# Key search: operands of VectorE's long products in a PSUM bank, unit tiles over two banks instead of four

## Chip, cores and metric

The kernel runs on one core of a Trainium2 chip. The metric is the device time of one execution in microseconds (us), from three runs. A core has five engines here: PE (matmuls), ACT (ScalarE), DVE (VectorE), POOL (GpSimd), and SP, which only issues transfers. SBUF is the large on-chip memory. PSUM holds eight banks of 128 x 512 float32 values, into which PE writes.

## What is computed

The reference is a transformer-like block (attention, a state space branch, cross attention, a product-key expert layer, and a second block after it). The change lies in the expert layer:

```python
def peer_ffn(a, w_q, sub_keys, u_tab, v_tab):      # 256 tokens, d = 1024
    qry = (af @ w_q).reshape(n, PEER_HEADS, 2, PEER_KEY_DIM)              # 8 heads, 2 halves
    s = jnp.einsum('nhpd,hpkd->nhpk', qry, sub_keys)                     # 128 keys a half
    s_top, i_top = lax.top_k(s, PEER_TOPK)                               # best 16 of 128
    cand = (s_top[:, :, 0, :, None] + s_top[:, :, 1, None, :]).reshape(n, PEER_HEADS, 256)
    sc, ci = lax.top_k(cand, PEER_TOPK)                                  # best 16 of 256 pairs
    e_a = jnp.take_along_axis(i_top[:, :, 0], ci // PEER_TOPK, axis=-1)
    e_b = jnp.take_along_axis(i_top[:, :, 1], ci % PEER_TOPK, axis=-1)
    experts = e_a * PEER_N_KEYS + e_b
    gw = jax.nn.softmax(sc, axis=-1)
    ...  # act = gelu(u_tab[experts] . x);  out = sum (gw * act) * v_tab[experts]
```

The kernel doesn't gather experts. It computes the activation of all 16384 experts for all tokens, multiplies by a dense matrix of gates, and sums with all rows of v_tab.

## The kernel before

**Unit tiles.** The 16384 experts are 128 tiles of u_tab, 128 experts each. A tile is a weight of 128 x 1024 float32. It arrives in a ring of four slots (SP's transfers). To keep float32 precision it is split in two: ACT copies it to a rounded `w_hi` (`split_high`), and another engine forms the rest `w_lo` = tile - `w_hi` (`split_rest`). `w_hi` and `w_lo` have two buffers each. PE then does 24 matmuls for the tile (`split_channels`): 16 with `w_hi` ("high"), and 8 with `w_lo` ("rest"), before which it waits for the rest. ACT takes the result out of the PSUM bank with a Gelu (`unit_out`), and SP stores it to HBM.

**Three loops.** The unit tiles run as loop `u1` (52 tiles, `U_EARLY`), loop `u2` (64 tiles, between which PE also builds the gate matrix, job `w`), and loop `u3` (12 tiles). In `u1` the rests are made by POOL (line 834 of the profile), so that DVE is free for the key search. In `u2` and `u3` DVE makes them (line 2170). `plan_banks` fixes the bank of every PSUM job in advance, and the counts of fills and releases on which PE, ACT and DVE wait. In `u1` the tiles rotate over banks 4, 5, 6, 7, in `u2` over 4, 5. Before `u1`, the jobs `sk` (key scores) and `ce` use banks 4 to 7. After `u1` come `eTr` (the turned expert numbers and gates, banks 6 and 7) and `cH` (banks 4 and 5).

**Order on ACT in u1.** For each tile `unit_out` of tile j comes first and `split_high` of tile j + 2 next. After 48 tiles (`U_EXP`) ACT does two small exponentials for the gates (`gate_exp`), with a change of its function table on either side.

**The key search on DVE.** For each half t of the tokens: `best_keys(t)` finds the best 16 of 128 for 16 groups, `best_pairs(t)` adds them to 256 pairs a head (`CAND`), finds the best 16 of those, and turns their places into expert numbers by one-hot products of 2048 values a partition; `gate_scores(t)` subtracts the best score. Between `best_keys(0)` and `best_pairs(0)` DVE does one product for another branch (line 2625: `CKK` by `CEX`, 2048 values). `gates(t)` waits for ACT's exponentials. `step(...)` makes DVE wait for its own last instruction. All these operands stand in `arena`, which is SBUF; PSUM shows as `banks` in the profile. Line 2580 is the sum for `CAND`, line 2594 the comparison, line 2595 the product with the numbers, line 2596 the sum over the one-hot axis, line 2600 the subtraction in `gate_scores`.

Of the kernel before, what the change touches and what calls it, by code (L numbers as in the profile page):

```python
# [21 lines left out]
P = 128  # L22
# [18 lines left out]
PH, PK, PTOP = 8, 128, 16  # L41
# [10 lines left out]
ALU = mybir.AluOpType  # L52
# [82 lines left out]
U_EARLY, U_EXP, U_GATED = 52, 48, 64  # L135
# [65 lines left out]
def plan_banks():  # L201
    B = Banks()
# [52 lines left out]
    for k in range(len(groups) + 1):  # L255
# [14 lines left out]
        if k >= 1:  # L270
            c, g = groups[k - 1]
# [61 lines left out]
    for d in range(2):  # L333
        for t in range(TT):
            B.job("ce", d, t, bank=4 + 2 * d + t)
    B.loop("u1", U_EARLY // 4, 4, banks=(4, 5, 6, 7))
    for t in range(TT):
        B.job("eTr", t, bank=6 + t)
    for d in range(2):
# [85 lines left out]
def bc(ap, axis, n):  # L425

    ap = ap.unsqueeze(axis)
    shape = list(ap.shape)
    shape[axis] = n
    return ap.to_broadcast(shape)  # L430
# [23 lines left out]

def build(nc, A):
    B = plan_banks()
    with ExitStack() as ctx:
        where = {}
# [13 lines left out]
        ps = ctx.enter_context(nc.psum_tensor("banks", [P, 8, 512], F32))  # L472
# [78 lines left out]
        def C(name):  # L551
            o, w = CONST[name]
            return const[:, o:o + w]
# [9 lines left out]
        def area(off, *dims):  # L563
            n = int(np.prod(dims))
            assert off + n <= 32768, (off, dims)
            v = arena[:, off:off + n]
            if len(dims) == 1:
                return v
            names_ = "abcd"[:len(dims)]
            return v.rearrange(f"p ({' '.join(names_)}) -> p {' '.join(names_)}",  # L570
                               **{k: d for k, d in zip(names_[1:], dims[1:])})
# [94 lines left out]
        CAND = area(10240, PH, 256)  # L666
# [2 lines left out]
        OH = area(14336, 2048)  # L669
        TOPV = area(16384, 16, PTOP)  # L670
        TOPI = area(16640, 16, PTOP)
        TOPIF = area(16896, 16, PTOP)
        SCV = area(17152, PH, PTOP)
        SCI = area(17280, PH, PTOP)
        CIA = area(17408, 2, P)
        CIAF = area(17664, 2, P)
        EAB = area(31744, TT, 3, P)
        SMX = area(18304, TT, PH)
        KEYS = area(18432, 16, P)
# [1445 lines left out]
        def _(dve):  # L2125
            V = nc.vector
            step = Chain(dve, S["dve_step"])
            ts, tt, stt, cp = V.tensor_scalar, V.tensor_tensor, V.scalar_tensor_tensor, V.tensor_copy

            def signal(ins, name, wait=None):  # L2130

                ins.then_inc(S[name], 1)
                if wait is not None:
                    dve.wait_ge(S[name], wait)
# [40 lines left out]
            for h in range(2):  # L2175
                k = slice(4 * h, 4 * h + 4)
# [41 lines left out]
            for s, (q, shift) in enumerate(((0.0, 0.0), (0.25, float(np.pi / 2)))):  # L2218
                k = ROPET[:, 1 + s, 0:48]
# [46 lines left out]
            for t in range(TT):  # L2266
                for a, b, hd, heads, f0 in ((0, 1280, DH, 10, 0), (1280, 1600, IDH, 5, 16)):
                    z_rests(*(((2,), (3, 4, 5)), ((6, 7, 8), (9, 10, 11)))[t][f0 > 0])
                    half = hd // 8
                    x = TOK[:, t, a:b].rearrange("p (h d) -> p h d", d=hd)  # L2270
# [3 lines left out]
                    n = heads * half  # L2274
# [224 lines left out]
            for h in range(2):  # L2499
                k = slice(4 * h, 4 * h + 4)  # L2500
# [50 lines left out]
            def top16(groups, src, work, val, idx):  # L2551

                for g in groups:
                    ins = V.max(val(g)[:, 0:8], src(g))
                step(ins)
                for g in groups:
                    V.max_index(idx(g)[:, 0:8], val(g)[:, 0:8], src(g))
                    ins = V.match_replace(out=work(g), in_to_replace=val(g)[:, 0:8], in_values=src(g),
                                          imm_value=TAKEN)
                step(ins)  # L2560
                for g in groups:
                    ins = V.max(val(g)[:, 8:16], work(g))
                step(ins)
                for g in groups:
                    ins = V.max_index(idx(g)[:, 8:16], val(g)[:, 8:16], work(g))
                step(ins)

            idxu = TOPI.bitcast(U32)
            sciu = SCI.bitcast(U32)
            ciau = CIA.bitcast(U32)  # L2570
# [5 lines left out]
                      lambda g: idxu[:, g, :])  # L2576

            def best_pairs(t):
                v = TOPV.rearrange("p (h x) k -> p h x k", x=2)
                step(tt(CAND.rearrange("p h (i j) -> p h i j", j=PTOP), bc(v[:, :, 0, :], 3, PTOP),  # L2580
                        bc(v[:, :, 1, :], 2, PTOP), ALU.add))
                top16(range(PH), lambda g: CAND[:, g, :], lambda g: CAND2[:, g, :], lambda g: SCV[:, g, :],
                      lambda g: sciu[:, g, :])

                flat = sciu.rearrange("p h k -> p (h k)")
                ts(ciau[:, 0, :], flat, 4, None, ALU.logical_shift_right)
                ts(ciau[:, 1, :], flat, 15, None, ALU.bitwise_and)
                step(cp(TOPIF, idxu))
                step(cp(CIAF, ciau))
                num = TOPIF.rearrange("p (h x) k -> p h x k", x=2)  # L2590
                oh4 = OH.rearrange("p (h k j) -> p h k j", h=PH, k=PTOP)
                oh3 = OH.rearrange("p (s j) -> p s j", j=PTOP)
                for x in range(2):
                    step(tt(oh3, bc(CIAF[:, x, :], 2, PTOP), bc(C("iota16"), 1, P), ALU.is_equal))
                    step(tt(oh4, oh4, bc(num[:, :, x, :], 2, PTOP), ALU.mult))
                    step(V.tensor_reduce(EAB[:, t, x, :], oh3, AX.X, ALU.add))

            def gate_scores(t):
                g3 = EAB[:, t, 2, :].rearrange("p (h k) -> p h k", h=PH)
                signal(tt(g3, SCV, bc(SCV[:, :, 0], 2, PTOP), ALU.subtract), "gate_sc")  # L2600

            def gates(t):
                g3 = EAB[:, t, 2, :].rearrange("p (h k) -> p h k", h=PH)
# [18 lines left out]
            for d in range(2):  # L2622
                for t in range(TT):
                    freed(dve, ("ce", d, t))
            signal(tt(CKK, CKK, CEX, ALU.mult), "ctx_kd")
            best_pairs(0)
            gate_scores(0)
            best_keys(1)
            best_pairs(1)
            gate_scores(1)  # L2630
            gates(0)
            gates(1)
# [4 lines left out]
            with dve.Fori(0, T // 16) as i:  # L2637
                for u in range(4):
                    split_rest(UD + u, "lo_ready", i, 4)
                    b, n = B.at[("w", (u - 2) % 4)]  # L2640
# [112 lines left out]
            for t in range(TT):  # L2753
                b = arrived(dve, ("sg", t)).rearrange("p (h n) -> p h n", h=HH)
                v = PJ[:, t, 512:1024]
# [325 lines left out]
```

## Time and profile before

| | us |
|---|---|
| median of 3 runs | 1853.91 (1852.71 to 1854.54) |
| the profiled execution, its own time | 1853.56 |
| its span, first to last instruction | 1851.7 |
| PE busy | 1790.3 (97%) |
| DVE busy | 1284.6 (69%) |
| ACT busy | 922.4 (50%) |
| POOL busy | 516.8 (28%) |

A busy PE counts every matmul from start to its modelled end, and matmuls overlap, so 97% doesn't mean that PE is at its peak. Loop `u1` lies between about 638 us and 799 us of the span, the key search between 626 us and 759 us, `u2` after 803 us.

### The profile page before, as it was taken

Reading aid. Unit: us, or ns where it says so; the run is one execution under the profiler, and the core shown is the slowest. Engines: PE = TensorE matmul, PEld = TensorE weight load, DVE = VectorE, ACT = ScalarE, POOL = GpSimd, SP = SyncE. Lnnn points to the kernel's source line nnn. Section 1 sums busy time; section 2 is a strip of 40 time slices with the busy share of each in tenths; the row PEclk is TensorE's granted clock in tenths of the full one; section 3 lists DMA queues with packets and bytes.
Section 4 is the critical chain, followed back from the end, with each engine's and each line's share of the span. In section 5 each row is a group of like instructions: output and inputs, shape, how many; then the busy total and the mean of one; then the engine's idle time right before and its main releaser. Section 6 shows DMA issues by size and latency. Waiting matters only on the chain.

```text
span 1851.7 us, 33113 instructions
## 1 busy us (share of the span) xinstructions
PE 1790.3 (97%) x11292; PEld 1563.7 (84%) x11292; DVE 1284.6 (69%) x2406; ACT 922.4 (50%) x1297; POOL 516.8 (28%) x232
## 2 busy tenths in 40 slices
PE   9999999999999989999999999999999999889997
PEld 6799977897978989999999988888887676559996
DVE  4567497777424499357777578888887785657777
ACT  5466444544556534477777543333334574234444
POOL 5157743600568598810000000000000000003333
PEclk9999999999999999999999999999999999999999
DMA  6554432578344467766555687777677781255553
GB/s 215 197 185 148 160 119 95 181 242 267 130 163 154 136 187 223 205 180 180 173 172 176 196 263 236 234 239 236 233 238 255 257 272 42 70 180 184 187 184 114
DMA packets 122841, 347.66 MB, mean 188 GB/s; under 512 B 13904, under 2 KB 46800, under 8 KB 122512
## 3 DMA queue, kind: packets, MB, share of 16 engines
q1 hardware_dynamic: 121248, 339.52, 57.1%
q0 software_dynamic: 1520, 7.21, 1.1%
q8 instruction: 41, 0.67, 0.1%
q14 instruction: 32, 0.26, 0.0%
HBM read 328.84 MB, written 17.83 MB: 187 GB/s over the span
## 4 chain that ended last, share of the span: by engine, by line
PE 80%; DVE 8%; POOL 4%; issue 3%; ACT 3%; DMA 2%; POOLq 0%; DVEq 0%; ACTq 0%; SPq 0%
PE banks L927 78%; POOL weight_rest L834 4%; DMA weight_ring<-in_stream 2%; ACT weight_high L1589 1%; PE banks L938 1%; DVE weight_rest L2170 1%; ACT arena L1589 1%; DVE ssd_rest L2196 1%; DVE arena L2397 1%; DVE arena L2922 0%; DVE attention_rest L2456 0%; ACT scratch L1589 0%; DVE arena L2346 0%; DMA residual<-in_x 0%; DVE arena L2211 0%
## 5 line engine op out<-in xcount | busy, mean ns | idle before, releaser
L1589 ACT ACTIVATE weight_high<-weight_ring 128x1024 fp32r<-128x1024 f32 x448 | 473.1, 1057 | 463.7 <-PE banks L927 364.1
L834 POOL TENSOR_TENSOR weight_rest<-weight_ring,weight_high 128x1024 fp32r<-128x1024 f32 x165 | 431.3, 2625 | 235.8 <-ACT weight_high L1589 152.4
L2170 DVE TENSOR_TENSOR weight_rest<-weight_ring,weight_high 128x1024 fp32r<-128x1024 f32 x283 | 346.2, 1224 | 202.6 <-ACT weight_high L1589 157.4
L927 PE MATMUL banks<-a_high,weight_high 128*128 128x256 f32 x1216 | 303.9, 288 | 0.1
L927 PE MATMUL banks<-a_rest,weight_high 128*128 128x256 f32 x1216 | 297.7, 283 | 0.0
L927 PEld LDWEIGHTS banks<-a_high,weight_high 128*128 128x128 f32 x1216 | 232.5, 191 | 1.5 <-issue 1.1
L927 PEld LDWEIGHTS banks<-a_rest,weight_high 128*128 128x128 f32 x1216 | 232.9, 192 | 0.3 <-issue 0.2
L927 PE MATMUL banks<-weight_high,gated_high 128*128 128x512 f32 x512 | 201.4, 393 | 0.0
L927 PE MATMUL banks<-weight_high,gated_rest 128*128 128x512 f32 x512 | 200.2, 391 | 0.0
L927 PE MATMUL banks<-a_high,weight_rest 128*128 128x256 f32 x1216 | 171.9, 284 | 12.4 <-POOL weight_rest L834 12.4
L927 PE MATMUL banks<-x_high,weight_high 128*128 128x256 f32 x672 | 167.1, 286 | 4.7 <-DVE x_rest L2891 3.7
L927 PEld LDWEIGHTS banks<-a_high,weight_rest 128*128 128x128 f32 x1216 | 156.6, 192 | 15.3 <-POOL weight_rest L834 15.3
L927 PE MATMUL banks<-x_rest,weight_high 128*128 128x256 f32 x672 | 165.8, 284 | 0.0
L1589 ACT ACTIVATE arena<-banks 128x512 f32<-128x512 f32 (+4 forms) x208 | 141.3, 703 | 35.0 <-PE banks L927 30.9
L927 PE MATMUL banks<-weight_rest,gated_high 128*128 128x512 f32 x512 | 140.2, 395 | 0.0
L1589 ACT ACTIVATE small<-banks 128x256 f32<-128x256 f32 x128 | 49.0, 383 | 175.7 <-PE banks L927 175.7
L927 PEld LDWEIGHTS banks<-x_high,weight_high 128*128 128x128 f32 x672 | 129.3, 192 | 7.0 <-ACT x_high L1589 3.9
L927 PEld LDWEIGHTS banks<-x_rest,weight_high 128*128 128x128 f32 x672 | 129.5, 193 | 1.3 <-issue 0.5
L927 PEld LDWEIGHTS banks<-weight_high,gated_high 128*128 128x128 f32 x512 | 96.3, 188 | 23.3
L927 PEld LDWEIGHTS banks<-weight_rest,gated_high 128*128 128x128 f32 x512 | 96.3, 188 | 21.4
L927 PEld LDWEIGHTS banks<-weight_high,gated_rest 128*128 128x128 f32 x512 | 96.1, 188 | 21.6
L2922 DVE SCALAR_TENSOR_TENSOR arena<-banks,cols,arena 128x189 f32<-128x189 f32 (+2 forms) x176 | 76.0, 432 | 46.4 <-ACT arena L1589 25.6
(316 smaller groups left out, 3167.3 us busy)
## 6 DMA issues: line engine op xcount, KB each, us to landing
weight_ring<-in_stream SPq DMA_DIRECT2D x512, 512.0 KB, 3.5
arena<-in_stream SPq DMA_DIRECT2D x66, 512.0 KB, 3.3
unit_spill<-small SPq DMA_DIRECT2D x128, 128.0 KB, 3.6
scratch<-unit_spill SPq DMA_DIRECT2D x128, 128.0 KB, 3.2
residual<-in_x SPq DMA_DIRECT2D x2, 512.0 KB, 4.2
arena<-in_mem POOLq DMA_DIRECT2D x2, 512.0 KB, 5.0
arena<-in_ctx POOLq DMA_DIRECT2D x2, 512.0 KB, 4.7
arena<-in_keys POOLq DMA_DIRECT2D x1, 1024.0 KB, 5.1
```

What stands on the lines that cost most here:

```text
L834: nc.gpsimd.tensor_tensor(w_lo[:, e % 2, :], raw(e)[0], w_hi[:, e % 2, :], ALU.subtract).then_inc(S["rest_ready"], 1)
L927: return nc.tensor.matmul(out, lhsT, rhs, start=start, stop=stop, skip_group_check=True)
L938: ins = nc.tensor.transpose(b[:, k * P:(k + 1) * P], src, ident)
L1589: return nc.scalar.activation(out, in_, f, **kw)
L2170: tt(w_lo[:, e % 2, :], raw(e)[0], w_hi[:, e % 2, :], ALU.subtract).then_inc(S[ready], 1)
L2196: tt(lo_[q], (actT if src is None else src)[q], hi[q], ALU.subtract).then_inc(S[ready], 1)
L2397: ins = ts(EM[:, k % 2, 4 * half + j, :], b[:, hsl(j)], ACS[:, c, h:h + 1], 0.0, ALU.subtract, ALU.min)
L2922: ins = stt(o[:, ro, wo], x[:, ri, wi], tap(k), o[:, ro, wo], ALU.mult, ALU.add)
```

## The change

The best values, the places, the key numbers and the scores, over which the long products of the search run, are written to PSUM bank 6 (`SEARCH`) by copies. In each product one operand is read from there, and the other from SBUF. Two copies for each half of the tokens are new (`TOPS`, `SCORES`); the two casts of before now write to PSUM (`NUMBERS`, `PLACES`). Bank 6 is made free for it: loop `u1` rotates over banks 4, 5, 4, 5. `gate_scores` now also waits for its own result, since the next half writes to the same place of the bank.

```diff
-    B.loop("u1", U_EARLY // 4, 4, banks=(4, 5, 6, 7))
+    B.loop("u1", U_EARLY // 4, 4, banks=(4, 5, 4, 5))
...
-        TOPIF = area(16896, 16, PTOP)
-        CIAF = area(17664, 2, P)
+        SEARCH = ps[:, 6, :]
+        TOPS = SEARCH[:, 0:256].rearrange("p (g k) -> p g k", g=16)
+        PLACES = SEARCH[:, 0:256].rearrange("p (x n) -> p x n", x=2)
+        NUMBERS = SEARCH[:, 256:512].rearrange("p (h x k) -> p h x k", h=PH, x=2)
+        SCORES = SEARCH[:, 0:128].rearrange("p (h k) -> p h k", h=PH)
...
             def best_pairs(t):
-                v = TOPV.rearrange("p (h x) k -> p h x k", x=2)
-                step(tt(CAND.rearrange("p h (i j) -> p h i j", j=PTOP), bc(v[:, :, 0, :], 3, PTOP),
-                        bc(v[:, :, 1, :], 2, PTOP), ALU.add))
+                pairs = lambda ap: ap.rearrange("p (h x) k -> p h x k", x=2)
+                step(cp(TOPS, TOPV))
+                step(tt(CAND.rearrange("p h (i j) -> p h i j", j=PTOP), bc(pairs(TOPS)[:, :, 0, :], 3, PTOP),
+                        bc(pairs(TOPV)[:, :, 1, :], 2, PTOP), ALU.add))
...
-                step(cp(TOPIF, idxu))
-                step(cp(CIAF, ciau))
-                num = TOPIF.rearrange("p (h x) k -> p h x k", x=2)
+                step(cp(NUMBERS.rearrange("p h x k -> p (h x) k"), idxu))
+                step(cp(PLACES, ciau))
...
                 for x in range(2):
-                    step(tt(oh3, bc(CIAF[:, x, :], 2, PTOP), bc(C("iota16"), 1, P), ALU.is_equal))
-                    step(tt(oh4, oh4, bc(num[:, :, x, :], 2, PTOP), ALU.mult))
+                    step(tt(oh3, bc(PLACES[:, x, :], 2, PTOP), bc(C("iota16"), 1, P), ALU.is_equal))
+                    step(tt(oh4, oh4, bc(NUMBERS[:, :, x, :], 2, PTOP), ALU.mult))
                     step(V.tensor_reduce(EAB[:, t, x, :], oh3, AX.X, ALU.add))
...
-                signal(tt(g3, SCV, bc(SCV[:, :, 0], 2, PTOP), ALU.subtract), "gate_sc")
+                step(cp(SCORES, SCV))
+                signal(tt(g3, SCORES, bc(SCV[:, :, 0], 2, PTOP), ALU.subtract), "gate_sc", t + 1)
```

## Rows read from the trace of the kernel before

**Rows 1.** Chain that ended last: start us, us, what; last rows from 780 us on.

```profile
756.20 27.16 PE banks L927 x224
...
799.17 0.14 issue
799.31 0.52 PE banks L938 x3
799.83 100.21 PE banks L927 x854
```

**Rows 2.** Chain that ended last, 860 us to the end.

```profile
859.92 584.20 PE banks L927 x3415
```

**Rows 3.** Busy us of each engine in stretches of the search, clock, DMA share, GB/s.

```profile
740.00:760.00 20.00, 16.07 (x127) 15.47 (x128) 18.49 (x6) 6.66 (x10) 19.08 (x7) 1.00 0.57 167
760.00:780.00 20.00, 20.00 (x169) 20.00 (x168) 0.00 (x0) 9.32 (x14) 16.75 (x8) 1.00 0.80 230
```

**Rows 4.** Who waited for whom, 640 to 790 us: total us, times, longest us.

```profile
PEld banks L927 <- POOL weight_rest L834: 13.0, 11, 1.5
```

**Rows 5.** Weight loads of the rests in time: start us, us, [idle before].

```profile
647.63 1.03 PEld L927 LDWEIGHTS banks<-a_high,weight_rest 128*128 128x128 f32 x8
651.49 1.01 PEld L927 LDWEIGHTS banks<-a_high,weight_rest 128*128 128x128 f32 x8 [0.91 <-POOL weight_rest L834]
655.87 1.01 PEld L927 LDWEIGHTS banks<-a_high,weight_rest 128*128 128x128 f32 x8 [1.45 <-POOL weight_rest L834]
...
756.20 1.02 PEld L927 LDWEIGHTS banks<-a_high,weight_rest 128*128 128x128 f32 x8 [1.46 <-POOL weight_rest L834]
...
759.06 1.03 PEld L927 LDWEIGHTS banks<-a_high,weight_rest 128*128 128x128 f32 x8
...
782.10 1.03 PEld L927 LDWEIGHTS banks<-a_high,weight_rest 128*128 128x128 f32 x8
```

**Rows 6.** Line 834 on POOL, 644.6 to 756 us: ns min/median/max, first and last start.

```profile
L834 POOL TENSOR_TENSOR weight_rest<-weight_ring,weight_high x34: 2397/2412/4425, 644.6 to 751.7; 128x1024 fp32r<-128x1024 f32 x34
```

**Rows 7.** POOL in time, from 644 us on.

```profile
644.64 2.41 POOL L834 TENSOR_TENSOR weight_rest<-weight_ring,weight_high 128x1024 fp32r<-128x1024 f32 x1 [0.56 <-ACT weight_high L1589]
647.44 4.00 POOL L834 TENSOR_TENSOR weight_rest<-weight_ring,weight_high 128x1024 fp32r<-128x1024 f32 x1 [0.39 <-ACT weight_high L1589]
651.41 4.42 POOL L834 TENSOR_TENSOR weight_rest<-weight_ring,weight_high 128x1024 fp32r<-128x1024 f32 x1
```

**Rows 8.** DVE in time, from 645 us on.

```profile
645.77 3.43 DVE L2625 TENSOR_TENSOR arena<-arena 128x2048 f32<-128x2048 f32 x1
649.12 4.47 DVE L2580 TENSOR_TENSOR arena<-arena 128x2048 f32<-128x2048 f32 x1
...
656.85 0.41 DVE L2558 MATCH_REPLACE8 arena<-arena 128x256 f32<-128x256 f32 x1
...
669.78 0.28 DVE L2588 CAST arena<-arena 128x256 f32<-128x256 uint32 x1
```

**Rows 9.** DVE's long products by line: ns min/median/max, first and last start.

```profile
L2594 DVE TENSOR_TENSOR arena<-arena,const x4: 4379/4381/4385, 670.4 to 745.1; 128x2048 f32<-128x2048 f32 x4
L2595 DVE TENSOR_TENSOR arena<-arena x4: 4357/4362/4365, 674.8 to 749.5; 128x2048 f32<-128x2048 f32 x4
L2596 DVE TENSOR_REDUCE arena<-arena x4: 2286/2286/2286, 679.2 to 753.9; 128x128 f32<-128x2048 f32 x4
L2600 DVE TENSOR_TENSOR arena<-arena x2: 2382/2390/2398, 692.7 to 756.3; 128x128 f32<-128x128 f32 x2
```

**Rows 10.** DVE in time, an earlier stage, 235 to 238 us.

```profile
235.03 0.67 DVE L2360 TENSOR_TENSOR arena<-banks,small 128x512 f32<-128x512 f32 x1
235.63 0.67 DVE L2361 TENSOR_TENSOR arena<-banks,rows 128x512 f32<-128x512 f32 x1
236.40 1.30 DVE L2366 TENSOR_TENSOR arena<-arena,small 128x512 f32<-128x512 f32 x1
```

**Rows 11.** POOL in the same stretch.

```profile
234.73 2.42 POOL L834 TENSOR_TENSOR weight_rest<-weight_ring,weight_high 128x1024 fp32r<-128x1024 f32 x1 [1.12 <-ACT weight_high L1589]
```

**Rows 12.** The same lines of DVE over the span: ns min/median/max.

```profile
L2366 DVE TENSOR_TENSOR arena<-arena,small x4: 692/693/1296, 236.4 to 275.6; 128x512 f32<-128x512 f32 x4
...
L2360 DVE TENSOR_TENSOR arena<-banks,small x8: 674/680/683, 233.8 to 274.2; 128x512 f32<-128x512 f32 x8
```

**Rows 13.** All engines in time, the end of u1, 788 to 800 us.

```profile
789.25 0.28 DVE L2605 TENSOR_REDUCE arena<-arena 128x8 f32<-128x128 f32 x1 [30.59 <-ACT arena L1589]
...
790.72 0.38 ACT L1589 ACTIVATE small<-banks 128x256 f32<-128x256 f32 x1
...
791.00 1.05 ACT L1589 ACTIVATE weight_high<-weight_ring 128x1024 fp32r<-128x1024 f32 x1
...
798.78 0.39 ACT L1589 ACTIVATE small<-banks 128x256 f32<-128x256 f32 x1 [1.55 <-PE banks L927]
...
799.31 0.52 PE L938 MATMUL banks<-const,arena 128*128 128x128 f32 x3 [0.30 <-ACT small L1589]
```

## The prediction

> **What bounds the kernel now.** I read the chain that ended last first. From 799.83 us to 900 us, and from 859.92 us for 584.20 us more, it is PE alone, without one wait [rows 1, 2]. So whatever makes `u1` end earlier reaches 1444 us whole, and behind that nothing of the change is left that could take it back. The question is what `u1` is bound by. The table of stretches shows it: from 760 to 780 us, when the search is over, PE is busy for 20.00 of 20 us; from 740 to 760 us, under DVE's last long products, for 16.07 us, while POOL rises to 19.08 us of 20 [rows 3]. The view of who waited for whom names it: 11 waits of PE's weight loads for POOL's rests, 13.0 us in all [rows 4].
>
> The size of the loss comes from the pace of the tiles. Free of waits, the eight weight loads of a rest start at 759.06 and, eight tiles on, at 782.10 us: 23.04 / 8 = 2.88 us a tile. From 647.63 to 756.20 us there are 33 tiles, since POOL makes 34 rests whose first (644.64 us) is used at 647.63 and whose last is used at 756.20 [rows 5 to 7]. They take 108.57 us where 33 x 2.88 = 95.04 would do. **The search costs PE 13.53 us.**
>
> How it costs them: POOL's rest takes 2.41 us, and under the products up to 4.42 us [rows 6, 7]. DVE's products of 2048 values take 4.36 to 4.38 us, while its reduction over the same 2048 takes 2.29 [rows 9]. The two take turns: at 645.77 us DVE starts L2625 under a POOL tile that runs until 647.05; 647.05 + 2.29 is 649.34, near its end at 649.20. POOL's tile started at 647.44 then needs 2.41 us more and ends at 651.44 [rows 7, 8]. So a product with both operands in SBUF and a POOL tile exclude each other for whole instructions. Even the subtraction of 128 values takes 2.39 us, about one POOL tile [rows 9]. POOL with 2.41 us of work in 2.88 can bear a hold of about 0.58 us (its tile is ready at 647.05, used at 647.63 [rows 5, 7]), not one of 2.29.
>
> **Step 1, one operand in a bank.** An earlier stage has both kinds of product under one POOL tile. POOL runs from 234.73 us for 2.42 us, its undisturbed length, while DVE does products with one operand in `banks` and one in SBUF: 0.67 us each, also undisturbed. Then, at 236.40, the product with both in SBUF takes 1.30 us instead of 0.69: it waited for the tile to end at 237.15 [rows 10 to 12]. The bank operand takes neither part of the exclusion. Each of the ten long products (two sums, four comparisons, four products) and both subtractions has one bank operand after the change. I take it that none of them holds POOL. What stays is L2625, which keeps both operands in SBUF and ends before the first copy. Its loss is the interval 647.63 to 651.49, 3.86 - 2.88 = 0.98 us. Behind it POOL would start at 651.44 and be done at 653.85, before PE's use at 651.49 + 2.88 = 654.37, so nothing more is lost. Gain: 13.53 - 0.98 = **12.55 us**. Bounds: nothing at all (if a 2048-value product behaved as now), and 13.53 (if the shift spared L2625's loss too). I take 12.55, since rows 10 to 12 show the same operation on the same two engines.
>
> On DVE the products would fall from 4.4 to about 2.3 us. The bank operand itself adds nothing: 680 ns against 693 for 512 values [rows 12]. Where DVE is later or earlier costs or gives nothing, because it waits 30.59 us at 789.25 for ACT's exponentials, which stand behind tile 48 on ACT [rows 13].
>
> **Step 2, the copies.** Per half of the tokens there are one new copy of 256 values, one of 128, and two casts that now end in PSUM. No row has a copy into PSUM. Nearest: the cast of 256 values at 0.28 us, and a replacement over 256 at 0.41 [rows 8]. On DVE the four copies are 4 x 0.41 and the four casts grow by 4 x 0.13, 2.2 us; if each of the eight had to wait for a POOL tile, 8 x 2.41 = 19.3 us more. Both lie under the 30.59 us, and the four comparisons and four products of 4.4 us alone give back 8 x 2.1 = 17 of it. On POOL a hold of 0.41 fits in the 0.58 of cover: 0. If that cover were gone, the four new copies would cost 4 x 0.41 = 1.6 us. I take 0 and keep 1.6 for the range. The Trainium skill (VectorE: DVE Perf Modes, "Why PSUM operands drop a tier") says that a two-port copy needs both SBUF read ports and that a PSUM operand rules it out. By it the copies would run at one value a cycle and never hold POOL, so the 1.6 us could not come. No run here shows such a copy.
>
> **Step 3, two banks instead of four.** PE may start tile j + 2 when ACT has emptied tile j's bank. ACT does that 0.39 us job before it makes `w_hi` of tile j + 2, and PE needs that `w_hi` anyway. So the new wait always ends at least 1.05 us before an older one. So it is at the table change too: tile 48 is out of its bank at 791.10, and the next `w_hi` is done at 792.05 [rows 13]. `u2` rotates over 4, 5 already and PE runs there without a wait [rows 1]. Cost 0. If the cover were gone, it would be 0.39 us a tile.
>
> The claims around the loop shift too. `eTr` of the second half used bank 7 right behind the last unit tile and waited for ACT to empty it: 0.30 us idle of PE [rows 13]. Bank 7 now has no unit tile, so that wait goes. The job `cH` on bank 5 inherits it, but comes after `eTr`, when the bank (799.17) is long free. Gain **0.30 us** (none to 0.5). The added wait in `gate_scores` queues `best_keys(1)` for the end of a 128-value operation, under 0.3 us on DVE, hidden as above. The waits at the table change (790 to 795 us) stay.
>
> **Sum.** 1853.56 - 12.55 - 0.30 = 1840.71 us for an execution like the profiled one. The median before lies 0.35 us above that execution's own time: **1841.0 us**, 0.7% faster. A measurement here tells about 0.2% (3.7 us) from no change.
>
> **Rivals.**
> - *The bank operand doesn't help long products.* Then stalls and lengths stay, only step 3's 0.30 us comes: 1853.6 us, within 0.2%. For it: no row has 2048 values or a spread (stepless) operand in a bank. Against it: rows 10 to 12. 4%.
> - *Part of it stays:* the copies hold POOL (+1.6), or the sums for `CAND`, the first users of the bank, still collide (the interval 651.49 to 655.87, 4.38 - 2.88 = 1.50 us [rows 5], and a smaller one in the second half, between none and as much): 1842.5 to 1844.5 us. 9%.
> - *The transfers become the bound.* Without stalls `u1` runs at 230 GB/s and a DMA share of 0.80 for 150 us, not for 27 [rows 3]. For it: 0.80 leaves little. Against it: in 756 to 783 us ten tiles in a row ran at 2.88 with no wait for the ring [rows 1, 5]. If each further tile came 0.15 us late, 33 x 0.15 = 5 us: 1846 us. 2%.
> - *Slower:* the two-bank rotation exposes ACT's emptying. 52 x 0.39 = 20.3 us, less the 12.9 gained: 1861.3 us. It decides only where ACT empties a bank later than one whole tile (2.88 us) after it is full; the one place with ACT so late is the table change, where `w_hi` is later still. From 0.25 us a tile on it would eat the gain. 2%.
> - The forecast: 83%.
>
> **Numbers.** The forecast's own range is 1839.9 (13.53 and 0.5 gained) to 1842.2. With the spread of single runs (1.2 us below the median) and the partial case above, the range is 1838.8 to 1844.5; it leaves out the transfers, the rival of no change and the slower one. Faster by over 0.2% (below 1850.2): the forecast, the partial case and the transfers, 0.94. Same: 0.04. Slower: 0.02.
>
> **What the changed profile would show.** Right: line 834 at 2.41 us throughout except one tile of about 4.0 us near 647; waits of PE for POOL in 640 to 790 us down from 11 to one of about 0.9; products with `banks` of about 2.3 us; DVE done near 738 us and idle for nearly 40 us; ACT's exponentials near 776 us; the 799.31 start of `eTr` without idle time before it. Wrong: POOL tiles of 4.4 us under products that read `banks`; PE waiting for `small` (a bank) inside `u1`; ACT waiting for the ring there. The likeliest way to miss is a hold that depends on something else than the two SBUF inputs, such as the spread operands.

## The result and the profile after

In the first comparison the changed kernel takes 1837.93 us (median of 4 runs, 1836.79 to 1842.40) against 1853.31 us of the one before: ratio 0.9929, 95% interval 0.9918 to 0.9941. (This ratio and those below are not quotients of medians; here that quotient is 0.9917, or 15.4 us less.) The forecast of 1841.0 from 1853.91 us is a ratio of 0.9930. The median by itself lies 0.9 us under the range of 1838.8 to 1844.5; the ratio times 1853.91 us is 1840.7 us. A second comparison, with five runs of the changed kernel, gave 0.9921 (0.9908 to 0.9935).

The profiled execution is the longest of the first four (1842.40 us, span 1840.6 us), so its end is no good measure. The length of loop `u1` is one.

The new lines shift the numbers: 834 is now 837 (POOL's rest), 927 is 930 and 938 is 941 (PE), 2580 is 2584 (sum for `CAND`), 2594 is 2597 (comparison), 2595 is 2598 (product), 2600 is 2604 (subtraction), 2605 is 2609, 2625 is 2629. Lines 2583 and 2603 are new copies into the bank. PEld is PE's loading of weights.

First the busy table of the changed kernel, over two stretches at and behind the end of the search as it was before (columns as in [rows 3]: busy us of PE, PEld, DVE, ACT and POOL, granted clock, DMA share, GB/s):

```profile
740.00:760.00 20.00, 20.00 (x169) 20.00 (x168) 0.00 (x0) 9.22 (x15) 16.68 (x8) 1.00 0.75 228
760.00:780.00 20.00, 19.80 (x165) 19.60 (x164) 1.53 (x6) 12.14 (x19) 15.08 (x8) 1.00 0.78 223
```

DVE is idle from 738 us on, and PE is busy for 20.00 us where it was for 16.07 [rows 3]. The waits in the loop, from the view of who waited for whom, 640 to 790 us:

```profile
DVE arena L2609 <- ACT arena L1592: 38.4, 1, 38.4
...
PEld banks L930 <- POOL weight_rest L837: 1.4, 2, 0.9
...
PEld banks L930 <- ACT weight_high L1592: 0.4, 1, 0.4
```

Of 11 waits for POOL (13.0 us [rows 4]) one of 0.9 is left, and one of 0.5 that belongs to the table change and lay just outside that window before. DVE waits 38.4 us for ACT, so that nothing of its own time counts. The weight loads of the rests in time:

```profile
647.47 1.03 PEld L930 LDWEIGHTS banks<-a_high,weight_rest 128*128 128x128 f32 x8
651.34 1.01 PEld L930 LDWEIGHTS banks<-a_high,weight_rest 128*128 128x128 f32 x8 [0.92 <-POOL weight_rest L837]
654.20 1.03 PEld L930 LDWEIGHTS banks<-a_high,weight_rest 128*128 128x128 f32 x8
...
755.00 1.03 PEld L930 LDWEIGHTS banks<-a_high,weight_rest 128*128 128x128 f32 x8
```

From 651.34 to 755.00 us there are 36 tiles at 2.88 us, without a wait: the interval of 4.38 us that stood at 655.87 [rows 5] is gone. The cause in DVE's and POOL's rows, in time, then by line (ns min/median/max):

```profile
645.60 3.43 DVE L2629 TENSOR_TENSOR arena<-arena 128x2048 f32<-128x2048 f32 x1
648.96 0.41 DVE L2583 COPY banks<-arena 128x256 f32<-128x256 f32 x1
649.40 2.29 DVE L2584 TENSOR_TENSOR arena<-banks,arena 128x2048 f32<-128x2048 f32 x1
```

```profile
647.28 4.01 POOL L837 TENSOR_TENSOR weight_rest<-weight_ring,weight_high 128x1024 fp32r<-128x1024 f32 x1 [0.39 <-ACT weight_high L1592]
...
651.25 2.39 POOL L837 TENSOR_TENSOR weight_rest<-weight_ring,weight_high 128x1024 fp32r<-128x1024 f32 x1
```

```profile
L2597 DVE TENSOR_TENSOR arena<-banks,const x4: 2291/2291/2293, 669.0 to 730.7; 128x2048 f32<-128x2048 f32 x4
L2598 DVE TENSOR_TENSOR arena<-arena,banks x4: 2286/2286/2289, 671.4 to 733.0; 128x2048 f32<-128x2048 f32 x4
...
L2604 DVE TENSOR_TENSOR arena<-banks,arena x2: 291/291/291, 683.3 to 738.0; 128x128 f32<-128x128 f32 x2
```

The product at line 2629 (2625 before) still waits for a POOL tile and makes the next one 4.01 us long. The sum behind it, with `banks` among its inputs, takes 2.29 us instead of 4.47. It runs beside the second part of that POOL tile and the start of the next, which takes 2.39 us. All four comparisons and all four products keep 2.29 us (4.38 and 4.36 before [rows 9]), and the subtraction 0.29 (2.39). The new copy of 256 values is 0.41 us.

The end of `u1`: PE in time, and the start of PE's unbroken run in the chain that ended last:

```profile
785.87 0.82 PE L941 MATMUL banks<-const,arena 128*128 128x128 f32 x6
```

```profile
786.69 644.16 PE banks L930 x3928
```

The six transposes of `eTr` run in one piece. **A measure of `u1` free of the rest of the program** is the time from the rest that starts near 647.5 us to the start of PE's unbroken run: 799.83 - 647.63 = 152.20 us before [rows 1, 5], 786.69 - 647.47 = 139.22 us after. That is 12.98 us gained, where the forecast had 12.85. The text below calls it the length of the stage.

### The profile page after: what moved, and what is told of

Same layout as the page of the kernel before. It is cut to its first block, busy times and chain, and to the rows that moved or that the text cites. A ratio compares the mean times of both kernels' runs of the same rounds, so it can differ in the third digit from the quotient of the medians.

```text
span 1840.6 us, 33171 instructions
## 1 busy us (share of the span) xinstructions
PE 1790.6 (97%) x11292; PEld 1565.6 (85%) x11292; DVE 1264.3 (69%) x2410; ACT 922.2 (50%) x1297; POOL 499.1 (27%) x232
## 4 chain that ended last, share of the span: by engine, by line
PE 85%; DVE 7%; ACT 2%; POOL 2%; issue 2%; DMA 1%; POOLq 0%; SPq 0%; DVEq 0%; ACTq 0%
PE banks L930 84%; POOL weight_rest L837 2%; PE banks L941 1%; DMA weight_ring<-in_stream 1%; ACT arena L1592 1%; ACT weight_high L1592 1%; DVE ssd_rest L2199 1%; DVE weight_rest L2173 1%; DVE arena L2400 1%; DVE arena L2926 0%; DVE attention_rest L2459 0%; DVE arena L2349 0%; DVE arena L2152 0%; ACT scratch L1592 0%; DVE arena L2407 0%
## 5 line engine op out<-in xcount | busy, mean ns | idle before, releaser
L837 POOL TENSOR_TENSOR weight_rest<-weight_ring,weight_high 128x1024 fp32r<-128x1024 f32 x165 | 413.6, 2515 | 240.8 <-ACT weight_high L1592 158.1
```

The costliest lines, as they stand in the source:

```text
L837: nc.gpsimd.tensor_tensor(w_lo[:, e % 2, :], raw(e)[0], w_hi[:, e % 2, :], ALU.subtract).then_inc(S["rest_ready"], 1)
```

## Experiments

Lengths of the stage, each from the two rows of its own trace, and ratios to the kernel before with their intervals:

| kernel | first rest, start of the run, us | stage, us | against the changed kernel, us | ratio |
|---|---|---|---|---|
| before | 647.63, 799.83 | 152.20 | +12.98 | 1 |
| changed | 647.47, 786.69 | 139.22 | 0 | 0.9929 (0.9918, 0.9941) |
| changed, again | 645.60, 784.82 | 139.22 | 0 | 0.9921 (0.9908, 0.9935) |
| rotation alone | 647.54, 799.36 | 151.82 | +12.60 | 0.9994 (0.9984, 1.0004) |
| one-hot operands in SBUF | 647.49, 796.89 | 149.40 | +10.18 | 0.9984 (0.9974, 0.9993) |
| six more sums, two SBUF inputs | 646.83, 794.47 | 147.64 | +8.42 | 0.9977 (0.9968, 0.9987) |
| six more sums, one from the bank | 646.03, 785.25 | 139.22 | 0.00 | 0.9921 (0.9899, 0.9943) |
| six more copies, SBUF to SBUF | 647.30, 788.74 | 141.44 | +2.22 | 0.9937 (0.9922, 0.9952) |
| one bank | 649.10, 826.75 | 177.65 | +38.43 | 1.0159 (1.0144, 1.0175) |
| last product through the bank | 647.89, 786.15 | 138.26 | -0.96 | 0.9920 (0.9906, 0.9934) |

**Rotation alone**, on the kernel before:

```diff
-    B.loop("u1", U_EARLY // 4, 4, banks=(4, 5, 6, 7))
+    B.loop("u1", U_EARLY // 4, 4, banks=(4, 5, 4, 5))
```

> The kernel before with one edit: loop u1 rotates over banks 4, 5, 4, 5; all operands of the search stay in SBUF. My theory (the two SBUF inputs of DVE's products and POOL's tiles exclude each other): the 11 waits of PE for POOL stay at 13.0 us, only the 0.30 us wait of the second eTr job for ACT goes: about 1853 us, the same within 0.2%. Rival 1 (the gain came from the banks, not from the operands): some 13 us faster. Rival 2 (the rotation itself costs, hidden behind the gain): PE waits for small inside u1, up to 0.39 us a tile, slower by up to 20 us.

The same within 0.2%, and the stage is 0.38 us shorter. The waits for POOL stay as they were in [rows 4]:

```profile
PEld banks L927 <- POOL weight_rest L834: 13.0, 11, 1.5
```

Rival 1 falls, and rival 2 too: no row has PE waiting for `small` there.

**One-hot operands in SBUF**, on the changed kernel:

```diff
-        PLACES = SEARCH[:, 0:256].rearrange("p (x n) -> p x n", x=2)
-        NUMBERS = SEARCH[:, 256:512].rearrange("p (h x k) -> p h x k", h=PH, x=2)
+        PLACES = area(17664, 2, P)
+        NUMBERS = area(16896, PH, 2, PTOP)
```

> The changed kernel with PLACES and NUMBERS back in SBUF, so that the four comparisons and four products have two SBUF inputs again; the sums for CAND and the subtraction keep their bank operand. My theory: the four pairs take 4.38 us an instruction again and cost PE what they cost before, 2.60 + 2.49 us in each half of the tokens, 10.2 us in all: 0.55% slower than the changed kernel, about 0.9984 of the one before; the sums stay at 2.29 us without a wait of PE. Rival (the bank operand helps only through some of the copies, or through the banks of the rotation): no loss, ratio 0.993.

The stage is 10.18 us longer than in the changed kernel, as expected (10.2), and the ratio is the expected 0.9984. DVE's groups and PE's waits, 640 to 790 us:

```profile
L2597 DVE TENSOR_TENSOR arena<-arena,const 128x2048 f32<-128x2048 f32 x4 | 17.5, 4381 | 0.1
L2598 DVE TENSOR_TENSOR arena<-arena 128x2048 f32<-128x2048 f32 x4 | 17.5, 4363 | 0.1
```

```profile
PEld banks L930 <- POOL weight_rest L837: 10.6, 9, 1.4
```

Nine waits: eight from the products and the one from line 2629. What is left of the gain, 12.60 - 10.18 = 2.42 us, is the share of the two sums and the subtractions; 4.38 - 2.88 = 1.50 us of it is the interval before 655.87 in [rows 5].

**Six more sums, two kinds of operands**, on the changed kernel, behind `gate_scores(1)`, where DVE was idle. The first reads both inputs from SBUF, the second one from the bank:

```diff
             gate_scores(1)
+            for _ in range(6):
+                step(tt(CAND2.rearrange("p h (i j) -> p h i j", j=PTOP), bc(TOPV.rearrange("p (h x) k -> p h x k", x=2)[:, :, 0, :], 3, PTOP),
+                        CAND.rearrange("p h (i j) -> p h i j", j=PTOP), ALU.add))
```

> The changed kernel with six more sums of 2048 values, both inputs in SBUF, on DVE after the search, where it was idle (their result goes to an area that nothing reads). My theory: each waits for a POOL tile and makes the next one wait, 4.38 us each; PE loses about 1.0 us at the first and 1.50 us at each further: 8.5 us (7.5 to 9.5), ratio to the kernel before about 0.9975. Rival (only DVE's own time matters, and it is hidden): nothing, ratio 0.993.

```diff
             gate_scores(1)
+            for _ in range(6):
+                step(tt(CAND2.rearrange("p h (i j) -> p h i j", j=PTOP), bc(NUMBERS[:, :, 0, :], 3, PTOP),
+                        CAND.rearrange("p h (i j) -> p h i j", j=PTOP), ALU.add))
```

> The same six more sums of 2048 values in the same place, with one input read from PSUM bank 6, spread over the last axis, and one from SBUF. My theory: 2.29 us each, POOL's tiles stay at 2.41, no wait of PE: ratio to the kernel before 0.993 as the changed kernel. Rival (a spread or long operand in a bank also excludes POOL, in part): PE loses between 0 and 8.5 us.

The pair differs in one operand's place and costs 8.42 us or 0.00. With two SBUF inputs, weight loads of the rests in time:

```profile
743.80 1.01 PEld L930 LDWEIGHTS banks<-a_high,weight_rest 128*128 128x128 f32 x8 [0.91 <-POOL weight_rest L837]
748.18 1.01 PEld L930 LDWEIGHTS banks<-a_high,weight_rest 128*128 128x128 f32 x8 [1.45 <-POOL weight_rest L837]
752.56 1.01 PEld L930 LDWEIGHTS banks<-a_high,weight_rest 128*128 128x128 f32 x8 [1.45 <-POOL weight_rest L837]
```

With one input from the bank, groups of 738 to 756 us:

```profile
L837 POOL TENSOR_TENSOR weight_rest<-weight_ring,weight_high 128x1024 fp32r<-128x1024 f32 x7 | 16.9, 2410 | 3.2 <-ACT weight_high L1592 3.2
L2636 DVE TENSOR_TENSOR arena<-banks,arena 128x2048 f32<-128x2048 f32 x6 | 13.7, 2291 | 0.2
```

4.38 us a tile in the one, tiles of 2.41 and sums of 2.29 us beside each other in the other. The bank operand is spread over the last axis, so spreading is no obstacle. The rival that only DVE's own time matters falls: with the two SBUF inputs DVE still waited 21.0 us for ACT's exponentials behind the sums, and PE lost 8.42 us all the same.

**Six more copies**, in the same place:

```diff
             gate_scores(1)
+            for _ in range(6):
+                step(cp(CAND2, CAND))
```

> The changed kernel with six copies of 2048 values from SBUF to SBUF on DVE after the search (the result is read by nothing): one input each. Theory A (DVE and POOL exclude each other also where a copy runs two values at a time, as the casts of 256 values in 0.28 us did): each copy is about 1.2 us long, waits for a POOL tile and holds the next one; POOL's pace becomes 2.41 + 1.2 = 3.6 us against PE's 2.88: 0.3 us lost at the first and 0.75 at each further, 4 us, ratio to the kernel before about 0.995. Theory B (only two SBUF inputs exclude POOL): copies of 1.2 us each, nothing lost, ratio 0.993.

Theory A was right in kind and wrong in size: 2.22 us instead of 4. The rests in time:

```profile
746.59 1.01 PEld L930 LDWEIGHTS banks<-a_high,weight_rest 128*128 128x128 f32 x8 [0.33 <-POOL weight_rest L837]
749.93 1.00 PEld L930 LDWEIGHTS banks<-a_high,weight_rest 128*128 128x128 f32 x8 [0.41 <-POOL weight_rest L837]
753.27 1.01 PEld L930 LDWEIGHTS banks<-a_high,weight_rest 128*128 128x128 f32 x8 [0.42 <-POOL weight_rest L837]
```

The pace is 3.34 us, so a copy holds POOL for 3.34 - 2.41 = 0.93 us and not for the estimated 1.2. Of six copies the first cost nothing, since POOL was idle for part of it. Five intervals are long, 0.40 + 4 x 0.46 = 2.24 us. The Trainium skill (SBUF — State Buffer, "Who interferes with whom") names both kinds that exclude GpSimd: two SBUF inputs, and the two-port modes of copies and casts. These runs agree that both kinds hold POOL, for 1.97 us (pace of 4.38 less 2.41) and 0.93 us at 2048 values. The page has the hold last for the whole instruction; measured, it is 1.97 us of the sum's 2.29. In which mode the copies ran, no run here shows.

**One bank for u1**, on the changed kernel:

```diff
-    B.loop("u1", U_EARLY // 4, 4, banks=(4, 5, 4, 5))
+    B.loop("u1", U_EARLY // 4, 4, banks=(4, 4, 4, 4))
```

> The changed kernel with loop u1 on bank 4 alone. It prices the wait that two banks were feared to expose. My theory: PE can start a tile only when ACT has emptied the bank of the tile before, 0.39 us and two hand-overs of some 0.1 us, so every tile takes 3.4 instead of 2.88 us: 51 x 0.5 = 26 us slower than the changed kernel, ratio to the kernel before about 1.007. The waits for POOL vanish, since it gets 0.5 us more a tile. Rival (PE hides the wait, or the wait for w_high is as long anyway): much less.

The wait exists and costs more than I reckoned, 38.43 us in the stage (ratio 1.0159 where 1.007 was expected). PE's loads, then ACT, then PE, in time:

```profile
700.57 1.03 PEld L930 LDWEIGHTS banks<-a_high,weight_rest 128*128 128x128 f32 x8
702.35 0.19 PEld L930 LDWEIGHTS banks<-a_high,weight_high 128*128 128x128 f32 x1 [0.75 <-issue]
```

```profile
701.85 0.38 ACT L1592 ACTIVATE small<-banks 128x256 f32<-128x256 f32 x1 [2.34 <-PE banks L930]
```

```profile
700.69 1.12 PE L930 MATMUL banks<-a_high,weight_rest 128*128 128x256 f32 x8
...
702.36 0.38 PE L930 MATMUL banks<-a_high,weight_high 128*128 128x256 f32 x1 [0.55 <-ACT small L1592]
```

The last matmul ends at 701.81, ACT empties from 701.85 to 702.23, and PE's next starts at 702.36. From the rest at 649.10 us to the one at 810.88 there are 44 tiles of 3.68 us, 0.80 over 2.88. Of that 0.55 us is the idle time shown. The rest, which my 0.5 us left out, is that matmuls of 0.28 us at a pace of 0.12 no longer overlap across the two tiles (0.16), and that the first one takes 0.38 us and the second starts 0.22 us behind it (0.10). These 44 tiles take 161.78 us against 127.69 in the changed kernel (647.47 to 775.16): 34.09 us more, which is 44 x 0.80 = 35.1 less the wait of about 1.0 us for POOL that is gone here, as expected. The other 4.34 us arise in the last tiles, at the change of ACT's function table, which I had not reckoned. There ACT empties the bank only behind the exponentials and both changes, PE sits idle for 1.89 us, and then its granted clock is 0.57 of the full one for some 4 us, near the lower of its two levels. PE's first matmul, and the busy table behind it:

```profile
814.00 0.38 PE L930 MATMUL banks<-a_high,weight_high 128*128 128x256 f32 x1 [1.89 <-ACT small L1592]
```

```profile
814.00:816.00 2.00, 2.00 (x10) 2.00 (x11) 0.00 (x0) 0.82 (x1) 1.10 (x1) 0.57 0.76 264
```

**The last product through the bank**, on the changed kernel:

```diff
-            signal(tt(CKK, CKK, CEX, ALU.mult), "ctx_kd")
+            for t in range(TT):
+                for d in range(2):
+                    half = slice(512 * d, 512 * d + 512)
+                    step(cp(SEARCH, CEX[:, t, half]))
+                    ins = tt(CKK[:, t, half], CKK[:, t, half], SEARCH, ALU.mult)
+                    signal(ins, "ctx_kd", 2 * t + d + 1)
...
-            pe.wait_ge(S["ctx_kd"], 1)
+            pe.wait_ge(S["ctx_kd"], 4)
```

> The changed kernel, and the one product left with two SBUF inputs (CKK by CEX) goes through bank 6 too: four copies of 512 values into the bank, each followed by a product with one bank operand. My theory: DVE needs 4 x (0.68 + 0.68) = 5.5 us instead of 3.4, hidden under its idle time of 38 us; POOL's tile of 4.0 us becomes 2.4 and PE's wait of 0.92 us at 651 us goes: 1.0 us faster than the changed kernel, too little for the times alone but plain in the profile. Rival (a copy into the bank holds POOL, 0.68 us each against a cover of 0.58): PE still waits, up to 0.5 us.

The stage is 0.96 us shorter; the rests start at 647.89, 650.77 and 653.65 us, 2.88 apart, with no wait. DVE and POOL in time:

```profile
646.75 0.69 DVE L2633 TENSOR_TENSOR arena<-arena,banks 128x512 f32<-128x512 f32 x1
647.47 0.69 DVE L2632 COPY banks<-arena 128x512 f32<-128x512 f32 x1
648.20 0.69 DVE L2633 TENSOR_TENSOR arena<-arena,banks 128x512 f32<-128x512 f32 x1
648.92 0.70 DVE L2632 COPY banks<-arena 128x512 f32<-128x512 f32 x1
```

```profile
647.70 2.41 POOL L837 TENSOR_TENSOR weight_rest<-weight_ring,weight_high 128x1024 fp32r<-128x1024 f32 x1 [0.40 <-ACT weight_high L1592]
```

So a copy from SBUF into a bank doesn't hold POOL, while one from SBUF to SBUF does. The times (0.9920 beside 0.9921 for the changed kernel) can't tell this version from the changed one; the stage can.

**The changed kernel again.**

> The changed kernel once more, beside the others on the same chip: 0.993 of the kernel before, and a second profile that shows whether the 2.2 us that its first profile lost behind 1515 us are there again. I expect them not to be: the granted clock there was 0.91 where that of the kernel before was 0.97, and the shift of 13.3 us should last to the end.

The ratio came, and the stage is again 139.22 us, but the expectation on the end was wrong. From the end of PE's unbroken run (1430.85 and 1428.97 us) to the end of the span the two profiles of the changed kernel take 409.8 and 409.5 us, that of the kernel before 407.6 (from 1444.12), the one with six more bank sums 405.5 (from 1429.41), and the one with six more copies 404.7 (from 1432.90), though the instructions of that part are the same in all.

## Why the prediction was right

- *What bounds `u1`.* PE, held up by POOL's rests under DVE's products, 13.53 us. Shown: taking eight of the ten products back brought 10.18 us of it back, and six new collisions cost 8.42 us against 8.5 expected. The last product through the bank brings the stage to 138.26 us; of the 152.20 - 138.26 = 13.94 us gained, 0.38 is step 3's, which leaves 13.56 beside the 13.53.
- *Step 1, 12.55 us.* Measured 12.98 - 0.38 = 12.60. The interval of 3.86 us that line 2625 was said to leave is 651.34 - 647.47 = 3.87, and the last product through the bank took 0.96 of it, near the 0.98 given. Two readings in it were rough. The exclusion doesn't last for whole instructions: a sum of 2.29 us adds 1.97 to POOL's pace. And the 0.58 us of cover holds for a single hold; where holds follow one another only 2.88 - 2.41 = 0.47 is covered, as the copies show (0.93 - 0.47 = 0.46 lost each). Neither changed the 12.55.
- *Step 2, 0.* Copies into the bank take 0.41 us (256 values) and 0.29 (128) and hold nothing. The 1.6 us kept for the range didn't come. The copies of 512 values into the bank left POOL at 2.41 us, those from SBUF to SBUF didn't. By this the rule of the Trainium skill (VectorE: DVE Perf Modes, "Why PSUM operands drop a tier") that the prediction cited agrees.
- *Step 3, 0.30 us.* Measured 0.38, and no wait for a bank in `u1`. That two banks cost nothing is shown by the rotation alone. That the order of ACT's work is the reason fits, but no run changed that order. One bank shows only that the wait is there when the bank needed is that of the tile just before: 0.80 us a tile. The rival's price of 0.39 a tile would have been too low by half: at 0.80 its 52 tiles are 41.6 us (an estimate), not 20.3. The cover at the table change was overstated too, by its own rows: 792.05 - 791.10 = 0.95 us, not 1.05.
- *Small signs.* DVE was done at 738.3 us (738 forecast), idle for 38.4 us; ACT's exponentials came at 776.26 (776).
- *The sums.* The terms give 1853.91 - 12.85 = 1841.06 us, and 1839.9 - 1.2 = 1838.7; the 1841.0 and 1838.8 printed are slips of rounding. For the 1842.2 no term is given.
- *What went wrong: that nothing happens to the shift behind 1444 us.* It is whole until 1430.85 us (13.27 us earlier than before, of which 0.16 us arose ahead of 647 us and 0.13 within the long run). Behind that, the profiled executions differ by up to 5 us, and the two of the changed kernel lost 1.9 and 2.2 us of the shift there. A spread of that size fits the single times of the changed kernel (1836.79 to 1842.40 us) and a median of 4 under the range, but only one execution of each set has a profile, so this is not shown. That the ratio came so near the forecast (0.9929, then 0.9921) is in part luck, since the end of the program varies by more than the 0.2 us between 0.9929 and 0.9930.

## What to carry to other kernels

When a DVE instruction takes about twice its length and a POOL instruction beside it too, look at where the inputs stand: moving one of two inputs to PSUM took away 12.6 us of PE's waiting, though the copies are added work for DVE. Ask what cover the held engine has per turn (here 2.88 - 2.41 = 0.47 us, where holds follow one another): PE lost only what a hold had above it, 0.46 of 0.93 us and 1.50 of 1.97. Measure a change of 1 us in the stage, between two instructions that no other variation touches, since the end of the program may vary by more than that.

## What was not expected of the hardware

Behind PE's unbroken run the same instructions took from 404.7 to 409.8 us. One part goes with the granted clock: busy tables of the 22 us behind the run, for the changed kernel and for that with six more bank sums:

```profile
1430.85:1452.85 22.00, 20.11 (x85) 14.16 (x86) 14.18 (x27) 9.87 (x12) 1.10 (x2) 0.92 0.75 267
```

```profile
1429.40:1451.40 22.00, 20.11 (x92) 14.33 (x92) 15.72 (x29) 11.05 (x15) 1.10 (x2) 1.00 0.80 276
```

0.92 of the full clock against 1.00, and 85 matmuls done against 92. The ten profiles fall in two groups by this number. At 1.00 the rest of the program took 404.7 to 405.6 us (rotation alone, one-hot operands in SBUF, and the three with six more operations). At 0.92 it took 407.1 to 409.8 us (the kernel before, both profiles of the changed one, one bank, the last product through the bank). Both groups have profiles with and without the operands in the bank, so it is not the change that brings it. The 0.92 is a mean over a short time at the lower of the two clock levels, in the changed kernel:

```profile
1438.85:1440.85 2.00, 2.00 (x6) 1.60 (x5) 2.00 (x3) 0.35 (x1) 0.00 (x0) 0.50 0.91 354
```

In the 8 us ahead of it PE was busy for the same time in both executions (4.00 of 4, 1.42 of 2 and 0.69 of 2 us), and yet the clock fell in one and stayed in the other. The rest lies in later dips and in waits for the ring's transfers (one of 6.34 us in the chain of the changed kernel). No run here settles what decides between the two, nor why the two profiles of the changed kernel are the longest.
